# Weight panels and operands ahead of squares and evictions at five stage borders, and a norm taken head by head

## The reference

```
h = x + 0.5 * swiglu(rmsnorm(h))                       # ffn 0: 1024 -> 2 x 2816 -> 1024
u = rmsnorm(h) @ w_mix_in                              # 1024 -> 3592
o = rmsnorm(gated_delta_rule(...), norm_w) * silu(z)   # 4 heads of 128, norm over a head
h = h + concat(short_conv(...), o) @ w_mix_out
h = h + 0.5 * swiglu(rmsnorm(h));  h = rmsnorm(h) * final_norm       # ffn 1
# second network, two layers: gated linear attention, then sparse attention (NSA)
h = h + concat(mixer(rmsnorm(h)), memory_attention) @ w_out[i]
h = h + conv_ffn(rmsnorm(h))     # u = x @ w_up; causal depthwise conv of width 3 over tokens;
                                 # silu(a) * b; @ w_down           (ffn 2 and ffn 3)
```

## Time and profile before

| | us |
|---|---|
| median of 3 runs | 2639.44 (2635.38 to 2646.66) |
| the profiled execution | 2635.17 |
| its span, first to last instruction | 2633.5 |
| TensorE busy in the span | 2476.2 (94%) |
| VectorE, ScalarE, GpSimd busy | 1338.2, 967.7, 149.4 |
| mean granted TensorE clock | 0.971 of full speed |

### The profile page before, as it was taken

One profiled execution on the slowest core, in us unless ns is written; L12 is line 12 of the kernel. 1 busy time (PEld: TensorE's weight loads), 2 busy tenths in 40 slices (PEclk: granted clock), 3 DMA queues, 4 the chain that ended last, 5 costly groups with the idle time before them and its releaser, 6 DMA issues.

```text
span 2633.5 us, 32260 instructions
## 1 busy us (share of the span) xinstructions
PE 2476.2 (94%) x12324; PEld 1999.1 (76%) x12324; DVE 1338.2 (51%) x2056; ACT 967.7 (37%) x1470; POOL 149.4 (6%) x132
## 2 busy tenths in 40 slices
PE   7999999989899999999999999998898878999996
PEld 6888876779778888867877788887776657788885
DVE  4444346575454443347655666633254773566633
ACT  4222237441442232253324333423234663433322
POOL 2000010022010000030001000001010001000001
PEclk9999999999999999999999999999898889999998
DMA  4333222210123333221112233323652102333321
GB/s 139 97 96 96 96 73 81 72 49 17 56 80 96 96 89 103 93 63 55 49 35 86 80 96 96 95 96 84 149 140 82 38 15 64 88 96 96 101 91 48
DMA packets 310548, 215.30 MB, mean 82 GB/s; under 512 B 40842, under 2 KB 294301, under 8 KB 310441
## 3 DMA queue, kind: packets, MB, share of 16 engines
q1 hardware_dynamic: 307176, 199.88, 26.3%
q0 software_dynamic: 3264, 13.94, 1.6%
HBM read 211.65 MB, written 8.44 MB: 84 GB/s over the span
## 4 chain that ended last, share of the span: by engine, by line
PE 82%; DVE 7%; ACT 6%; issue 2%; POOL 1%; DMA 1%; POOLq 0%; ACTq 0%; DVEq 0%
PE bank L504 16%; PE bank L506 16%; PE bank L505 16%; PE bank L644 6%; PE bank L643 6%; PE bank L642 6%; PE bank L817 2%; POOL rstd L763 1%; ACT arena L2567 1%; DVE arena L2493 1%; PE bank L2009 1%; ACT wH L381 1%; DVE wL L409 1%; PE bank L2400 1%; PE bank L1493 1%
## 5 line engine op out<-in xcount | busy, mean ns | idle before, releaser
L504 PE MATMUL bank<-xH,wH 128*128 128x512 f32 (+2 forms) x1992 | 798.4, 401 | 52.9 <-DVE xL L716 17.6
L506 PE MATMUL bank<-xH,wL 128*128 128x512 f32 (+2 forms) x1992 | 785.2, 394 | 0.0
L505 PE MATMUL bank<-xL,wH 128*128 128x512 f32 (+2 forms) x1992 | 784.8, 394 | 0.0
L409 DVE TENSOR_TENSOR wL<-raw,wH 128x1024 fp32r<-128x1024 f32 (+2 forms) x365 | 449.7, 1233 | 562.8 <-ACT wH L381 562.4
L381 ACT ACTIVATE wH<-raw 128x1024 fp32r<-128x1024 f32 (+2 forms) x365 | 379.0, 1039 | 828.0 <-PE bank L506 404.8
L504 PEld LDWEIGHTS bank<-xH,wH 128*128 128x128 f32 (+2 forms) x1992 | 374.0, 188 | 157.9 <-issue 36.7
L505 PEld LDWEIGHTS bank<-xL,wH 128*128 128x128 f32 (+2 forms) x1992 | 374.7, 188 | 86.4 <-issue 4.1
L506 PEld LDWEIGHTS bank<-xH,wL 128*128 128x128 f32 (+2 forms) x1992 | 373.9, 188 | 86.6
L644 PE MATMUL bank<-g_hi,wL 128*128 128x512 f32 x704 | 280.9, 399 | 0.0
L642 PE MATMUL bank<-g_hi,wH 128*128 128x512 f32 x704 | 276.3, 393 | 1.2 <-DVE wL L409 1.2
L643 PE MATMUL bank<-g_lo,wH 128*128 128x512 f32 x704 | 277.4, 394 | 0.0
(11 more groups left out here) (327 smaller groups left out, 2709.1 us busy)
## 6 DMA issues: line engine op xcount, KB each, us to landing
raw<-in_ffn_w_in SPq DMA_DIRECT2D x88, 512.0 KB, 3.8
raw<-in_w_up SPq DMA_DIRECT2D x88, 512.0 KB, 3.8
raw<-in_ffn_w_out SPq DMA_DIRECT2D x44, 512.0 KB, 3.5
raw<-in_w_down SPq DMA_DIRECT2D x44, 512.0 KB, 3.5
raw<-in_w_mix_in SPq DMA_DIRECT2D x28, 512.0 KB, 3.8
raw<-in_gla_w_in SPq DMA_DIRECT2D x16, 384.0 KB, 3.2
raw<-in_w_kv_shared SPq DMA_DIRECT2D x12, 512.0 KB, 6.5
rel_wide<-rel_rows POOLq DMA_DIRECT2D x12, 512.0 KB, 12.1
```

Source lines behind the costliest of these rows:

```text
L409: nc.vector.tensor_tensor(wL[:, h, 0:n], raw[:, k, 0:n], wH[:, h, 0:n].bitcast(F32), ALU.subtract)\
L504: pe.matmul(o, wh, xa, start=a, stop=False)
L505: pe.matmul(o, wh, xb, start=False, stop=False)
L506: last = pe.matmul(o, wl, xa, start=False, stop=z)
```

## The change

Seven edits:
- mix_out: two squares come before the copy of panel 2 (`first_squares`), two behind it. VectorE multiplies the unnormalised head by the gain and silu(z) while the norm is made. Then, head by head, ScalarE makes Exp, VectorE one product with it, ScalarE xH, VectorE xL.
- `refill_act`: four squares, the wait, all of xH, the other four squares.
- gla_rest: the 8 weighted squares are parted: 3 before mem0_kv's evictions, 3 behind the copy of panel 1, 2 behind the copy of panel 2.
- ffn2_up and ffn3_up: two new functions, `conv_up_act` and `conv_up_dve`, take the place of `dense_act` and `dense_dve`. In turn 0 panel 5 is split between the evictions of tiles 1 and 2, where it was behind all four. In later turns an eviction comes first and then the panel one further ahead; the sequence of panels and evictions is the same, but the loop's boundary, and with it `between`, lies one panel later.
- `conv_evac_act`: the taps of tiles 0 and 1 wait for the Silu of the turn before.

```diff
--- before.py
+++ after.py
@@ -513,6 +513,29 @@
             else:
                 turns(pe, s, body, peeled, between)
 
+        def conv_up_act(act, name, evac, between, hook, extra={}):
+
+            s = plan.stages[name]
+            n = len(s.panels)
+
+            def body(i):
+                if isinstance(i, int) and i == 0:
+                    for j in range(n):
+                        split_ahead(act, s, 0, j)
+                        if (0, j) in extra:
+                            extra[0, j]()
+                    hook()
+                    for t in range(n):
+                        evac(act, s, 0, t)
+                        if t == 1:
+                            split_ahead(act, s, 0, n)
+                    return
+                for j in range(n):
+                    evac(act, s, i, j)
+                    if not isinstance(i, int) or j < n - 1:
+                        split_ahead(act, s, i, j + 1)
+            turns(act, s, body, True, between)
+
         def dense_act(act, name, evac, between=None, late=0, hook=None, extra={}):
 
             s = plan.stages[name]
@@ -532,6 +555,29 @@
                     if fixed and (i, j) in extra:
                         extra[i, j]()
             turns(act, s, body, late > 0, between)
+
...
         def dense_dve(dve, name, evac, between=None, late=0, hook=None, extra={}):
 
@@ -1132,10 +1178,18 @@
             dense_act(act, "mix_z", nothing, extra={(0, 0): keys, (0, 1): lambda: chunk_out(0),
                                                     (0, 2): lambda: chunk_out(1), (0, 3): after_z})
 
-            def norms():
+            def first_squares():
                 chunk_out(3)
                 act.wait_ge(sem("o_mix"), 4)
-                for h in range(4):
+                for h in range(2):
+                    squares(act, 12 + h, H4[:, OT, h])
+
+            def head_hi(h):
+                act.wait_ge(sem("gdn_out"), 4 + h + 1)
+                nc.scalar.activation(xH[:, 4 + h, :], H4[:, OT, h], ACT.Copy).then_inc(sem("x_hi"), 1)
+
+            def norms():
+                for h in range(2, 4):
                     squares(act, 12 + h, H4[:, OT, h])
                 for h in range(4):
                     act.wait_ge(sem("sum_mix"), 12 + h + 1)
@@ -1143,12 +1197,10 @@
                       .then_inc(sem("norm_mix"), 1)
                 for h in range(4):
                     inverse_root(act, 12 + h, U[:, 20 + h, :])
-
-            def head_hi():
-                for h in range(4):
-                    act.wait_ge(sem("gdn_out"), 4 + h + 1)
-                    nc.scalar.activation(xH[:, 4 + h, :], H4[:, OT, h], ACT.Copy).then_inc(sem("x_hi"), 1)
-            dense_act(act, "mix_out", nothing, extra={(0, 0): norms, (0, 1): head_hi})
+                    if h:
+                        head_hi(h - 1)
+                head_hi(3)
+            dense_act(act, "mix_out", nothing, extra={(0, 0): first_squares, (0, 1): norms})
 
         def conv_dve(dve, t):
 
@@ -1341,22 +1393,28 @@
                              (0, 3): lambda: (new_values(2), state(2), short_lo(), new_values(3))})
 
             def gated():
+                dve.wait_ge(sem("z_silu"), 1)
+                for h in range(4):
+                    dve.wait_ge(sem("sq_mix"), 12 + h + 1)
+                    nc.vector.scalar_tensor_tensor(out=H4[:, OT, h], in0=H4[:, OT, h], scalar=column("gdn_out_norm"),
+                                                   in1=H4[:, Z, h], op0=ALU.mult, op1=ALU.mult)\
+                      .then_inc(sem("gdn_out"), 1)
+
+            def head_lo(h):
+                dve.wait_ge(sem("x_hi"), xbase(2) + 4 + h + 1)
+                nc.vector.tensor_tensor(xL[:, 4 + h, :], H4[:, OT, h], xHf[:, 4 + h, :], ALU.subtract)\
+                  .then_inc(sem("x_ready"), 1)
+
+            def normed():
                 for h in range(4):
                     dve.wait_ge(sem("inv_mix"), 12 + h + 1)
-                    nc.vector.scalar_tensor_tensor(out=H4[:, OT, h], in0=H4[:, OT, h], scalar=column("gdn_out_norm"),
-                                                   in1=U[:, 20 + h, :], op0=ALU.mult, op1=ALU.mult)\
+                    dve.wait_ge(sem("gdn_out"), h + 1)
+                    nc.vector.tensor_tensor(H4[:, OT, h], H4[:, OT, h], U[:, 20 + h, :], ALU.mult)\
                       .then_inc(sem("gdn_out"), 1)
-                dve.wait_ge(sem("z_silu"), 1)
-                for h in range(4):
-                    dve.wait_ge(sem("gdn_out"), h + 1)
-                    nc.vector.tensor_tensor(H4[:, OT, h], H4[:, OT, h], H4[:, Z, h], ALU.mult).then_inc(sem("gdn_out"), 1)
-
-            def head_lo():
-                for h in range(4):
-                    dve.wait_ge(sem("x_hi"), xbase(2) + 4 + h + 1)
-                    nc.vector.tensor_tensor(xL[:, 4 + h, :], H4[:, OT, h], xHf[:, 4 + h, :], ALU.subtract)\
-                      .then_inc(sem("x_ready"), 1)
-            dense_dve(dve, "mix_out", residual(1.0), extra={(0, 0): gated, (0, 1): head_lo})
+                    if h:
+                        head_lo(h - 1)
+                head_lo(3)
+            dense_dve(dve, "mix_out", residual(1.0), extra={(0, 0): gated, (0, 1): normed})
 
         def gdn_pool(pool):
             pool.wait_ge(sem("dec_exp"), 1)
@@ -2119,6 +2177,8 @@
             act.wait_ge(sem("evac_dve"), plan.evac(s, i, t))
             if t == 2:
                 act.wait_ge(sem("cv_prod"), 2 * k + CREDIT)
+            if t < 2 and (not isinstance(i, int) or k):
+                act.wait_ge(sem("cv_silu"), 2 * k - 1 + t)
             nc.scalar.activation(cv[:, t, :], us[:, t, :], ACT.Copy, scale=conv_columns(s, i, t)[2])\
               .then_inc(sem("cv_tap"), 1)
             if t >= 2:
@@ -2709,12 +2769,13 @@
         def refill_act(act, f, r, name):
 
             ready = h_from(name)
-            for k in range(KD - 1):
+            for k in range(4):
                 square(act, r, k, ready(k))
             act.wait_ge(*matmuls_done(name))
             for k in range(KD):
                 x_hi(act, f, k, ready(k))
-            square(act, r, KD - 1, ready(KD - 1))
+            for k in range(4, KD):
+                square(act, r, k, ready(k))
 
         @nc_block.scalar
         def _(act):
@@ -2739,11 +2800,15 @@
             act.wait_ge(sem("gain4"), 1)
             fill_act(act, 4, 3, h_from("ffn1_down"))
             split_first(act, "gla_rest")
-            for k in range(KD):
-                square(act, 4, k, h_from("ffn1_down")(k), column("final_norm", k))
+
+            def final_squares(first, end):
+                for k in range(first, end):
+                    square(act, 4, k, h_from("ffn1_down")(k), column("final_norm", k))
+            final_squares(0, 3)
             dense_act(act, "mem0_kv", evac_to("act", mem_place))
             dense_act(act, "gla_rest", nothing,
-                      extra={(0, 1): lambda: rstd_act(act, 3), (0, 2): lambda: rstd2_act(act)})
+                      extra={(0, 0): lambda: final_squares(3, 6),
+                             (0, 1): lambda: (final_squares(6, KD), rstd_act(act, 3)), (0, 2): lambda: rstd2_act(act)})
             dense_act(act, "gla_q", nothing,
                       extra={(0, 1): lambda: gate_abs_act(act),
                              (0, 2): lambda: (gate_exp_act(act), mem_round_act(act, 0, 0)),
@@ -2764,8 +2829,8 @@
                              **{(0, j): lambda j=j: (go_hi_act(act, 2 * j - 2), go_hi_act(act, 2 * j - 1))
                                 for j in range(1, 5)}})
             fill_act(act, 6, 5, h_from("gla_out"))
-            dense_act(act, "ffn2_up", conv_evac_act, lambda: (mem_norm_act(act, 1), g_first_act(act, 2)),
-                      late=4, hook=lambda: rstd_act(act, 5))
+            conv_up_act(act, "ffn2_up", conv_evac_act, lambda: (mem_norm_act(act, 1), g_first_act(act, 2)),
+                        hook=lambda: rstd_act(act, 5))
             down_act(act, 2)
             fill_act(act, 7, 6, h_from("ffn2_down"))
             split_first(act, "kv_f")
@@ -2783,7 +2848,7 @@
             attend_act(act)
             dense_act(act, "nsa_out", nothing)
             refill_act(act, 10, 7, "nsa_out")
-            dense_act(act, "ffn3_up", conv_evac_act, lambda: g_first_act(act, 3), late=4, hook=lambda: rstd_act(act, 7))
+            conv_up_act(act, "ffn3_up", conv_evac_act, lambda: g_first_act(act, 3), hook=lambda: rstd_act(act, 7))
             down_act(act, 3)
             for k in range(KD):
                 square(act, 8, k, h_from("ffn3_down")(k))
@@ -2843,8 +2908,8 @@
                                 for j in range(1, 4)},
                              (0, 4): lambda: (go_lo_dve(dve, 6), go_lo_dve(dve, 7))})
             residuals_dve(dve, "gla_out", 1.0, 6)
-            dense_dve(dve, "ffn2_up", conv_evac_dve, lambda: g_first_dve(dve, 2), late=4, hook=lambda: norm_dve(dve, 5),
-                      extra={(0, 1): lambda: mem_turn_dve(dve, 1)})
```

(24 more changed lines are left out.)

## The result

The changed kernel took 2614.9 us, median of six runs (2613.4 to 2616.5). The kernel before took 2643.0 in the six runs it now has (2635.4 to 2652.0). The ratio is 0.9907, 95% interval 0.9885 to 0.9929: faster by 0.7 to 1.2%. The profiled executions took 2614.86 and 2635.17 us, so 20.3 us went between them. The forecast was 2619 (2608 to 2630), and its sum against the profiled execution alone was 2614.5.

A forecast was written before the change was run, and what follows sets the result against it. TensorE, busy 94% of the span, bounds the kernel; its stalls and the clock lost behind them are the price. 6.1 + 5.7 + 5.9 + 4.8 - 1.8 = 20.7 us off the 2639.4 median gives 2619 us (2608 to 2630).

The forecast's parts named there:

- Part 1: First mixer's norm (mix_out): head-by-head order lets TensorE finish its first tile at 713.95 instead of 720.1; about -6.1 us.
- Part 2: Two refills (mix_out to ffn1_up, nsa_out to ffn3_up): earlier restart, but a new stall before tile 1; 0.9 us lost each.
- Part 3: ffn1_down to gla_rest: tile 1 starts 4.0 us earlier without a stall and 1.7 us of clock return; about -5.7 us.
- Part 4: Two ffn_up borders with convolution: sixth panel copied earlier, stall gone, clock back, 0.5 us lost at panel 6; -5.9 and -4.8.
- The premise on the clock: At the edited borders: stalls of 3.25 us or more bring the lower clock, 2.72 does not; 1.7 to 2.8 us lost.
- A: Rival: the two refills gain 4.4 us instead of losing 1.8; 27 us in all, 2612 us; chance 0.12.
- B: Rival: the clock falls all the same in parts 1, 3 and 4; gain 15 us, 2624 us; chance 0.14.
- C: Rival: the new waits slow the 18 turns of the ffn2_up and ffn3_up loops; +15 us, 2655 us; chance 0.03.
- D: Rival: gains are taken back later by a transfer or GpSimd's table work; 2632 us or more; chance 0.05.

The follow-up runs named there:

- e1: Kernel before with only mix_out's norm made head by head; 6.1 us gained at that border, 2627.6 us in all.
- e5: Changed kernel with the old refill order (seven squares, xH, one square); 1.1 and 1.35 us better at the two refills, span 2611.2 us.
- e2: Kernel before with only the parted weighted squares in front of gla_rest; 5.2 us gained at tile 1, span 2634.7 us.
- e6: Changed kernel with unread matmuls filling the stalls before tile 1 of ffn1_up (18) and ffn3_up (14); span 2615.6 us.
- e7: Changed kernel, but GpSimd's additions 6 and 7 in both refills wait for panel 1's wL; span 2617.3 us.
- e8: Changed kernel, but in both refills ScalarE copies panel 1 ahead of the last four squares; 5.0 and 5.1 us better there, span 2610.1 us.
- e9: e8 plus ffn1_up's memory-turn copies on VectorE moved behind panel 2's wL; median 2611.3 us, ratio to the kernel before 0.9895.
- e11: The kernel before run again, unchanged; 2635.9 us.
- e4: Kernel before with only the two added waits of a tap for the previous turn's Silu; 2636.5 us.

## Why the prediction was right, step by step

**Part 1, -6.1.** Measured 6.1 by itself (e1) and in the changed kernel. The first matmul on a head is at 710.26 (forecast 710.05, on the time of the kernel before, which is 0.20 earlier: nothing is off). The three waits between heads are 0.18, 0.24 and none, and the clock stayed at 1.00.

**Part 2, +0.9 each.** Measured +1.1 (e1 and e5) and +1.3 to 1.35 (difference over the border, e5). The mechanism is as written, the terms are not. In the second refill, on the time of the kernel before (16.26 us later), the last addition before the fourth square was forecast to end at 2233.9; here the square starts at 2218.26, which is 2234.5, because the two additions took 3.35 us (2214.81 to 2218.16) and not 2 x 1.43, beside the last two xL. The wL ended the stall at 2222.22, which is 2238.48. Tile 1 had started at 2238.69 before; the 2238.95 that the prediction names is the start of ScalarE's copy, which waits for tile 0's last matmul to be through. So 0.2 us were gained where 1.35 were forecast. The clock then took 0.20 x 7.8 = 1.6, where 2.25 is in the 0.9 (its range was 1.7 to 2.8). The two misses, 1.1 and 0.7 us, are of opposite sign, and that the net came within 0.5 us of 0.9 is in part luck. In the first refill 0.55 us were gained at tile 1 and 1.7 lost to the clock.

**Part 3, -5.7.** Measured 5.2: 3.95 for the stall (1149.57 against 1140.83, less the 4.79 already gained; 4.0 forecast), and the clock behind it gave 1.2 instead of 1.7. Alone (e2) the border gave the same 5.2.

**Part 4, -5.9 and -4.8.** Measured 6.2 to 6.35 and 5.2: 5.8 and 4.8 at the sixth panel, and 0.4 in each last turn, where 0.2 was forecast. The loss at panel 6 is less than the 0.5 priced in: in ffn2_up VectorE's wL for it waits 0.37 us for the copy, and TensorE loses 0.3 there and 0.1 in ffn3_up. No tile of the loops lies further apart than before.

**The sum.** 6.1 + 5.7 + 5.9 + 4.8 - 1.8 = 20.7 forecast, 20.3 measured between the profiled executions. The borders by themselves give 6.1 + 5.2 + 6.35 + 5.2 - 1.1 - 1.3 = 20.4. That the total agrees as well is luck: the clock's steps in stretches without an edit (-2.44, +2.25 and smaller ones) happened to cancel. In e2, e6, e7, e8 and e9 they did not, and with the losses at the start took 4 to 7 us from a local gain.

**Where the forecast was off.** It moved the sum onto the median of the runs, 4.3 us above the profiled execution, and so came to 2619 where 2614.9 was measured. That gap was taken as constant. The runs say otherwise: the 11 later runs of the kernel before go from 2631.7 to 2648.8 us, and their mean clock from 0.973 to 0.965; 0.008 of 2640 us is 21 us, which is about the 17 us of spread. The changed kernel's six go over 3 us in the first set (2613.4 to 2616.5) and over 1.5 in the last (2613.9 to 2615.4). By these numbers the gap was mostly lost clock, and the changed kernel has most of it no more. The medians of the two kernels differ by 28 us in the first set and by 24 in the last, against 20.3 for the profiled pair. Which stages lose the clock in the old kernel's slower runs, and whether the removed stalls are what let it scatter, stays open: both of its profiles are of runs of about 2635 us. e9 speaks against the removed stalls: it has shorter stalls at the refills than the changed kernel, and its six runs spread over 12 us (2610.2 to 2622.3, mean clock 0.974 to 0.968).

**The premise on the clock.** That every stall of 3.25 us or more is followed by the lower clock, and one of 2.72 is not, was read from the rows of the borders and is too sharp. e1 kept full speed behind 3.25, and 2.72 lost it in the changed kernel and in e11. The profile of the kernel before had a shorter stall with the lower clock behind it all along, in a stretch that the prediction did not look at. TensorE's timeline there, and the window of 6 us:

```profile
1309.06 5.44 PE L2009 MATMUL bank<-arena 96*128 96x128 f32 x32 [2.06 <-DVE arena L1972]
...
1309.00:1315.00 6.00, 5.95 (x35) 5.79 (x36) 2.58 (x4) 0.48 (x1) 0.00 (x0) 0.72 0.49 128
```

So the clock's part of each term (1.7 to 2.8 us) is what such a stall mostly costs, not always.

**The rivals.** A: both tiles start behind stalls of 4.17 and 3.43 us, and the refills cost. B: the clock kept full speed behind the heads, in gla_rest and in both ffn_up borders. C: nothing in e4. D: losses did come back later, but by the clock, not by a transfer or GpSimd, and in the changed kernel a gain (+2.25) stood against the loss (-2.44).

## What to carry to other kernels

Where one engine is busy 94% of the span, price a stall as its length plus what the clock loses behind it, and look at what stands in queue ahead of the operand that ends it: moving one panel copy in front of squares that another engine paces was worth 5 to 6 us a border, and putting those squares in front of the copy lost the whole restart that an earlier xH had won. Check a local edit at its own border by pairing the n-th matmul of both traces; the total of a single run holds several clock losses of 1.6 to 3.3 us that fall by chance. Keep the gap between the median and the profiled execution out of a sum, or say which side of it is clock.

## What the runs showed of the hardware

**A stall's length alone does not decide the clock behind it.** Counted over the 13 profiles of this study, before, after and e1 to e11, each time in the 6 us behind the stall: the stall of 2.72 us in front of line 504 (1929.33 before) was followed by the lower clock in 8 of 13. The one of 2.08 us ahead of the 32 matmuls in 4 of 13: 3.81 us where it was not, 5.44 (e9) to 7.07 (e2) where it was. The 3.25 us at the sixth panel of ffn2_up in 4 of the 5 kernels that have it; the two refills' stalls of 3.20 us and more in all. One of 3.03 to 3.18 us near 2150 to 2170, in 10 of 13. But the stall of 2.06 to 2.08 us that stands 18.6 us ahead of the one counted above, in front of 32 equal matmuls (1309.06 before), was followed by the lower clock in 13 of 13 (5.43 or 5.44 us for the 32), and the 2.31 to 2.33 us at the start of the second refill in all 6 kernels that have it. So at some places a short stall is a chance of losing 1.6 to 3.3 us and at others the loss is as sure as behind a long one; what tells these places apart stays open. The Trainium skill, "TensorE: Matmul & The Clock Gate", section "What's actually happening", says that the number of slow matmuls at the start of one and the same kernel differs from run to run. Behind a stall inside this kernel it did so too: 24 and 17 matmuls in the same 5.5 us in the two executions of the kernel before.

**VectorE and GpSimd slow each other in both directions.** In e8 four additions took 9.47 us (2.37 each) with wL and the memory turn beside them, in e9 6.81 and in the changed kernel 6.16. An addition with nothing beside it takes 1.28; the 1.43 of the earlier trace rows is a mean that has stretched ones in it. In GpSimd's timeline of e8, the four and then the third by itself, and in VectorE's the memory turn beside it:

```profile
752.38 9.47 POOL L810 TENSOR_TENSOR rstd<-rstd,sq 128x512 f32<-128x512 f32 x4 [4.96 <-ACT sq L773]
...
756.47 3.15 POOL L810 TENSOR_TENSOR rstd<-rstd,sq 128x512 f32<-128x512 f32 x1
...
756.17 2.31 DVE L1699 TENSOR_TENSOR arena<-arena 128x2048 f32<-128x2048 f32 x1
```

The memory turn ends at 758.48, and the addition, which began beside it, at 759.62, 1.14 later. The wL that starts next on VectorE (758.40) ends at 760.71, 1.09 after that addition. So the two take turns: each instruction ends about as long after the other engine's as it takes alone, a little less.
